# Output projection of an encoder layer: the order of the three products of the split operands over four PSUM banks

## What is computed

```
merged = sigmoid(ga) * (oa @ w_up_a) + sigmoid(gb) * (ob @ w_up_b)      # (512, 2048)
h      = x + merged @ w_out                                             # w_out: (2048, 2048)
y      = h + hier_moe(rms_norm(h, norm2_g))
```

## Time and profile before

| | us |
|---|---|
| median of 3 runs | 2326.51 |
| the three runs | 2326.81, 2326.51, 2323.01 |
| span of the profiled execution, first to last instruction | 2323.9 |
| execution time of the profiled execution | not given on its page |
| tensor engine busy, of the span | 2165.1 |
| the stage of the output projection in that execution | 1059.9 to about 1256 |

### The profile page before, as it was taken

The page is one execution under the profiler, slowest core; times in us unless marked ns, Lnnn a source line. Parts: engine busy times, 40 slices in busy tenths (PEclk is TensorE's granted clock), DMA queues, the critical chain, the costliest instruction groups (busy, mean ns, idle before and its releaser), DMA issues.

```text
span 2323.9 us, 31259 instructions
## 1 busy us (share of the span) xinstructions
PE 2165.1 (93%) x12178; PEld 1583.7 (68%) x12178; DVE 851.9 (37%) x1131; ACT 650.2 (28%) x816; POOL 67.4 (3%) x114
## 2 busy tenths in 40 slices
PE   5999999999999999999997699989988989888887
PEld 4888888888888888888886455555555555555554
DVE  4555454544222222224223433333333233333324
ACT  4446455453222222223322122212122112121121
POOL 1000000010000000000000000000000000000000
PEclk9999999999999999999998799999999999999998
DMA  5422222322333333336544599999999999999994
GB/s 178 124 82 77 86 88 76 95 78 86 95 99 96 94 99 97 92 99 195 198 147 162 195 410 408 407 415 411 408 407 399 405 410 414 405 397 410 415 388 179
DMA packets 264062, 541.99 MB, mean 233 GB/s; under 512 B 24856, under 2 KB 200152, under 8 KB 212696
## 3 DMA queue, kind: packets, MB, share of 16 engines
q1 hardware_dynamic: 260776, 532.57, 61.6%
q0 software_dynamic: 3248, 8.90, 1.4%
HBM read 541.93 MB, written 11.55 MB: 238 GB/s over the span
## 4 chain that ended last, share of the span: by engine, by line
PE 76%; DMA 15%; DVE 4%; issue 2%; ACT 1%; ACTq 0%; SPq 0%; DVEq 0%; POOL 0%; POOLq 0%
DMA wd_s<-in_w_down 14%; PE PS L1307 13%; PE PS L1309 13%; PE PS L1308 13%; PE PS L1637 10%; PE PS L1663 7%; PE PS L1622 5%; PE PS L1324 3%; PE PS L1326 3%; PE PS L1325 3%; PE PS L1612 2%; PE PS L1380 1%; DVE h L1237 1%; DVE y_lo L1275 1%; ACT y_hi L861 1%
## 5 line engine op out<-in xcount | busy, mean ns | idle before, releaser
L1019 DVE TENSOR_TENSOR w_lo<-w_raw,w_hi 128x1024 fp32r<-128x1024 f32 x200 | 245.0, 1225 | 673.0 <-ACT w_hi L585 673.0
L1307 PE MATMUL PS<-x_hi,w_hi 128*128 128x512 f32 x1088 | 431.2, 396 | 2.4 <-DVE x_lo L1012 2.4
L1309 PE MATMUL PS<-x_hi,w_lo 128*128 128x512 f32 x1088 | 424.6, 390 | 0.0
L1308 PE MATMUL PS<-x_lo,w_hi 128*128 128x512 f32 x1088 | 424.3, 390 | 0.0
L585 ACT ACTIVATE w_hi<-w_raw 128x1024 fp32r<-128x1024 f32 x200 | 211.8, 1059 | 703.6 <-PE PS L1309 574.9
L1637 PE MATMUL PS<-wu_s,xT 128*64 128x256 f32 x2048 | 312.4, 381 | 0.0
L1663 PE MATMUL PS<-wd_s,hT 128*64 128x512 f32 x1024 | 245.8, 631 | 33.5 <-DMA wd_s<-in_w_down 25.2
L1307 PEld LDWEIGHTS PS<-x_hi,w_hi 128*128 128x128 f32 x1088 | 204.6, 188 | 46.7 <-issue 3.0
L1308 PEld LDWEIGHTS PS<-x_lo,w_hi 128*128 128x128 f32 x1088 | 204.8, 188 | 43.5 <-issue 2.4
L1309 PEld LDWEIGHTS PS<-x_hi,w_lo 128*128 128x128 f32 x1088 | 204.6, 188 | 43.5
L1237 DVE TENSOR_TENSOR h<-h,PS 128x1024 f32<-128x1024 f32 x136 | 161.3, 1217 | 136.2 <-PE PS L1622 135.8
(11 more groups left out here) (222 smaller groups left out, 2314.5 us busy)
## 6 DMA issues: line engine op xcount, KB each, us to landing
wu_s<-in_w_up SPq DMA_DIRECT2D x128, 1024.0 KB, 25.6
wd_s<-in_w_down SPq DMA_DIRECT2D x128, 1024.0 KB, 25.2
w_raw<-in_w_in SPq DMA_DIRECT2D x136, 512.0 KB, 3.8
wg_s<-in_w_gate SPq DMA_DIRECT2D x64, 1024.0 KB, 26.7
wg_odd<-in_w_gate SPq DMA_DIRECT2D x64, 1024.0 KB, 28.5
w_raw<-in_w_out SPq DMA_DIRECT2D x32, 512.0 KB, 3.9
w_raw<-in_w_up_a SPq DMA_DIRECT2D x16, 512.0 KB, 3.9
w_raw<-in_w_up_b SPq DMA_DIRECT2D x16, 512.0 KB, 3.9
```

What stands on the lines that cost most here:

```text
L1019: V.tensor_tensor(w_lo[:, b, :], w_raw[:, r, :], w_hi[:, b, :].bitcast(F32), ALU.subtract).then_inc(s_wlo, 1)
L1307: mm(PS[:, bank, :], wh[:, k, :], rhs_hi[:, k0 + k, :], start=(start and k == 0), stop=False)
L1308: mm(PS[:, bank, :], wh[:, k, :], rhs_lo[:, k0 + k, :], start=False, stop=False)
L1309: last = mm(PS[:, bank, :], wl[:, k, :], rhs_hi[:, k0 + k, :], start=False, stop=(stop and k == 7))
```

## The change

For each feature tile `k` the loops over the products and over the token tiles are exchanged. Before, the three products of one token tile followed each other in one bank, then those of the next tile. Now the product `m_hi*w_hi` is issued for the four tiles (banks 0, 1, 2, 3), then `m_lo*w_hi` for the four, then `m_hi*w_lo`. The wait for `s_h` stands before the first product of its bank as it did; since the first products of the four banks now follow each other, so do the four waits. The matmuls are called directly and not through `three`; their operands, their number, the start and stop flags of each bank and the signal on the last matmul of a chunk (bank 3, product `m_hi*w_lo`) are the same.

```diff
                         k = 2 * c + kk
-                        for t in range(NT):
-                            if k == 0 and nn:
-                                pe.wait_ge(s_h, 4 * (nn - 1) + t + 1)
-                            a, b = m_hi[:, k, t * P:t * P + P], m_lo[:, k, t * P:t * P + P]
-                            last = three(PS[:, t, :], a, b, wh[:, kk, :], wl[:, kk, :], start=(k == 0), stop=(k == KT - 1))
+                        for part, (m, w) in enumerate(((m_hi, wh), (m_lo, wh), (m_hi, wl))):
+                            for t in range(NT):
+                                if k == 0 and nn and part == 0:
+                                    pe.wait_ge(s_h, 4 * (nn - 1) + t + 1)
+                                last = mm(PS[:, t, :], m[:, k, t * P:t * P + P], w[:, kk, :],
+                                          start=(k == 0 and part == 0), stop=(k == KT - 1 and part == 2))
                     last.then_inc(s_chunk, 1)
```

## The result

Over 15 runs each, the changed kernel takes 2328.84 us in the median (2324.37 to 2331.16), the kernel before 2324.88 us (2321.99 to 2327.86). The ratio is 1.0015, 95% interval [1.0008, 1.0022]: slower by 3.5 us, between 1.9 and 5.1. In a later comparison on one chip it was 1.0019 [1.0010, 1.0028]. The profiled execution has the forecast span to the figure shown on its page, 2327.3 us. That is partly luck, as its stages show. This window answers to the first of the earlier trace rows (length, busy of PE, PEld, DVE, ACT, POOL, granted clock, DMA share, GB/s). Its end is that of the earlier trace rows moved by the 3.4 us of the forecast and cuts the stage short: in this execution the last product of the stage starts at 1260.02.

A forecast was written before the change was run, and what follows sets the result against it. PE was taken to bound the projection stage; step 0 plus 3.4 us for three boundaries, added to 2326.51, gave 2329.9 us. Its own range was 2327 to 2332, the wider one 2324.5 to 2334.0.

The forecast's parts named there:

- The step at nothing: Projection matmuls: 512 more bank switches cost zero, the step staying 0.2267 us.
- The boundary at 1.12 us: Starts of stretches 1 to 3: waits for banks 1 to 3 no longer hidden, 1.12 us each, 3.4 in all.
- Nothing else is held up: Splits, ring transfers and h_add behind the later chunk signal: none delayed enough to make PE wait, no added cost.
- Passed on to the end in full: Routing, gather and experts start later by PE's delay, so the full 3.4 us reaches the end.
- The clock at a chance of 0.03: Rival: stops at each boundary drop the clock to 1.2 GHz, 2.7 us a boundary, 8.2 in all, 2338.1; chance 0.03.
- The rival of the hidden loss: Experts' weight stream, not PE, sets the end and starts as before, so the loss is taken up: 2326.5; chance 0.08.
- both of the switch: Rivals on projection bank switches: faster, 5.1 us saved, 2324.8, chance 0.10; or costing 4.5 us, 2334.4, chance 0.13.
- the switch's price: Rival: each projection product changing bank is 0.0058 us slower, 4.5 us in all, sum 2334.4; chance 0.13.

The follow-up runs named there:

- e2: Kernel before, with the changed order only in the first feature tile of stretches 1, 2 and 3 (36 of 768 products): ratio 1.0016 to before.
- e4: Kernel before, but each stretch's last chunk finishes bank after bank, h_add of banks 0 to 2 waiting for its own bank: 2316.56 us, 0.9962.
- e1: Changed kernel, but the first feature tile of stretches 1, 2 and 3 keeps the order of before: ratio 0.9998 to the kernel before.
- e6: e4 with the changed order in all chunks but the last of each stretch: 2320.00 us, 0.9980 to the kernel before.
- e7: e4 unchanged, run again on one chip with the repeat of e6: 2315.89 us, 0.9965 to the kernel before.
- e8: e6 unchanged, run again on one chip beside e7: 2318.34 us, 0.9971 to the kernel before.

## Why the prediction was right, point by point

- **The step at nothing: right.** 0.2267 us with a switch each time. The 0.22 of the earlier trace rows was rounding, and the 0.2325 of the earlier trace rows belongs to short groups behind a wait. The 11 ns over the figure of the Trainium skill ("TensorE: Matmul & The Clock Gate", section "Back-to-back issue gap") stay, whatever the order of the banks; the trace does not agree with a pace of 216 ns for these fp32r matmuls.
- **The boundary at 1.12 us, bounds 1.01 to 1.36: right,** 1.03 to 1.07 measured in twelve boundaries without a fall of the clock. The small excess is in the first step: I let each first product start 0.16 us behind the end of its `h_add`, so the fourth 1.81 behind the first. That holds for the first alone. The loads of the other three start at 1106.18, 1106.78 and 1107.38, so 0.50, 1.10 and 1.70 behind the first product at 1105.68: the fourth comes 0.11 sooner than I took it. The slower steps behind it give back about half of that.
- **Nothing else is held up: right.** The prediction took it from PE's lack of other waits before the change, which shows no margin. In the changed kernel PE still waits in these 768 products for `h_add` alone.
- **Passed on to the end in full: right.** e2 loses, and e4 wins, at the end of the run what their stages lose and win, within the intervals: 3.7 us by the ratio for 3.1, and 8.8 for 9.3. In the profiled execution it can't be read from the span. There the first expert starts 5.6 us later (1308.52 for 1302.92): 1.0 before the stage, 3.1 at the boundaries, 1.6 by the clock, 0.1 less elsewhere. The experts' loop was 2.2 shorter; over all thirteen traces it scatters between 1018.8 and 1022.9 us with no relation to the change. That the span came to 2327.3 is a sum of such accidents; the 15 runs are what bears out the 3.4. The absolute 2329.9 started from the median of three runs, 1.6 above that of fifteen, and so lies 1.1 above the 2328.84 measured.
- **The clock at a chance of 0.03: mis-sized.** The step that failed is "the trace does not bear it out for stops of this size". That was read from one stop of 0.94, and the change puts three more behind it. It fell at 3 of 15 such boundaries, for 1.6 us each and not 2.7. On the mean over those five traces that is 1.0 us on top of 3.1, which fits 3.5 and 4.4 (1.0015 and 1.0019) a little better than 3.1 alone, though the intervals hold both; it kept the result within the forecast's own range.
- **The rival of the hidden loss and both of the switch** are ruled out by e1, e2 and e4. The wider range of 2324.5 to 2334.0 was said to take in the switch's price, but that rival's own sum is 2334.4.

## What to carry to other kernels

When loops over banks and products are exchanged, don't ask only whether the matmuls keep their step; ask when each bank is asked for anew, and compare that with the pace at which the other engine frees them. One product a bank asks every 0.23 us, three ask every 0.69, and a VectorE that frees one every 0.60 fits between the two. Better than either order is to close the banks one after the other and let each be emptied alone: that gave 8 to 9 us where the exchanged loops lost 3.5. Of these, 5.6 are the boundaries and the shorter wait behind the last stretch; 3.3 came with the clock, which is not always so (e6).

## What the runs showed of the hardware beyond that

- Behind three stalls of 0.3 us that follow one of 0.94 the granted clock fell to its lower level at 3 of 15 boundaries (0.73 over 6.3 us), behind a single stall of 2.74 at two of three (0.75 and 0.76), behind one of 0.94 alone at none of nine; the same stalls left it at 1.00 elsewhere in the same execution.
- The stalls of 0.3 us are named as waits at the weight loads (0.35 to 0.41 us) and show in the distance of the starts, not as waits in the rows of PE.
- A shorter gap of PE before the router's small matmuls went along with more than its own gain in three of four traces (e4, e7, e8): 1.9 us less waiting and 3.3 us less in the products, at a clock of 1.00 for 0.62. In e6, with the same short gap, the clock was 0.63.
